# The bonus products of the chunked state stage write to bank XB0 in place of PB1

## The chip, the cores and the metric

The kernel runs on one core of a Trainium2 chip. The metric is the device time of one execution in microseconds; the number quoted is the median of several runs. The core's engines are named as the profile names them: PE is TensorE's matmul row and PEld its weight loads, DVE is VectorE, ACT is ScalarE, POOL is GpSimd, and SP is the queue that issues most of the transfers. Each engine works through its own list of instructions in order. They meet only at semaphores, counters on which one engine waits until another has raised them. Matmul results go to PSUM, which the kernel uses as banks of 128 partitions by 512 f32 values.

## The reference

One layer of a diffusion backbone over 2048 latent tokens and 256 context tokens of width 1024: a token mixer with two branches (retention and RWKV-7 time mixing, both in both directions), then a mixture of 16 experts. The change sits in the RWKV-7 branch. For every token `t` and each of 8 heads of width 64 the state is updated and read, and a per-head bonus is formed beside it:

```python
def step(s, xt):
    wt, kt, vt, kkt, at = xt[:5]
    sa = jnp.einsum('bhvk,bhk->bhv', s, -kkt)
    s = (s * wt[:, :, None, :] + sa[..., None] * (kkt * at)[:, :, None, :]
         + vt[..., None] * kt[:, :, None, :])
    ...
    return s, jnp.einsum('bhvk,bhk->bhv', s, xt[5])
...
u = lp['rwkv_w0'][:, None, None, :] + jnp.einsum('btr,drc->dbtc', jnp.tanh(wd), lp['rwkv_w2'])
a = jax.nn.sigmoid(lp['rwkv_a0'][:, None, None, :] + jnp.einsum('btr,drc->dbtc', ad, lp['rwkv_a2']))
...
bonus = jnp.sum(qu['r'][None] * st['k'] * r_k, axis=-1, keepdims=True).sum(0) * st['v']
```

The bonus is, for each token and head, a sum over the head's 64 channels of a product of three vectors. The kernel forms the product on POOL (`bon`) and takes the sum on PE, by a matmul against `ones2`, a matrix of two columns that mark the two heads of a block of 128 channels.

## The kernel before, in words

The function `rwkv_chunks` replaces the scan over tokens by work on chunks of 128 tokens. There are 18 chunks and two directions, so 36 halves. The prologue prepares the first chunk; then a loop of 18 passes runs two halves each (`d` = 0 and 1), and an epilogue finishes the last one. A half does two things at once. It inverts a triangular matrix for the chunk that was prepared, in six levels (`couple` and `double` on PE, `copies` on ACT, `levels` on DVE), and it prepares the next chunk of the other direction. The order on each engine is the order of the calls in its `body`, written out by hand. There is no planner; what an engine waits for is in its `wait_ge` calls.

All eight banks are in use: `XB[0]`, `XB[1]`, `TP[0]`, `TP[1]`, `TTP[0]`, `TTP[1]`, `PB[0]` and `PB[1]`. The end of a half and the start of the next one, which is what the change touches, go like this:

- On PE, `pairs` (L900) makes the products of the next chunk, two banks for each of four `q`: `XB`, then `PB`, then `XB` again, then `TTP`. DVE's `masked` (L778) empties each of the eight banks with one operation and raises `m1d` by one for it, so `m1d` 5 and 6 stand for the second use of `XB[0]` and `XB[1]`, and `m1d` 8 for all.
- PE's `turn` (L911) then transposes `beta` into `PB[0]`, `kappa` into `PB[1]` and `vS` into `PB[0]`. ACT's `turned` copies them out (`trc` 1, 2, 3).
- At the end of `turn`, PE sums the bonus (L916, eight small matmuls in the profile, since an f32 product takes two): it writes 8 columns of `PB[1]`, after waiting for `trc` 2 (the copy of `kappa_t` out of that bank) and for POOL's `bon`.
- PE's `low_rank` computes `u` into `PB[0]` (L874) and `a` into `PB[1]` (L879) for the chunk after the next. Before L879 it waits for `bonc`, which ACT raises when it has copied the 8 columns into `bo`.
- PE's `inverse_seed` starts the next half: for each group of four heads it adds `TTb` into `TP[g]` (L932) and `TTP[g]` (L934). DVE makes `TTb` in `seeds` (L782, L784) from ACT's copy `ATb`.
- PE's `couple` (L941) multiplies into `XB[0]` and `XB[1]`, each after ACT's copy `Tb` of that group.

On ACT the same stretch reads: `ATb` of group 0, `beta_t`, `kappa_t`, `v_t`, `ATb` of group 1, `bo`, then `rates` (a table load and the sigmoid `sg` out of `PB[0]`, and the sigmoid `av` out of `PB[1]`, L609 and L612), then `copies(0)`, the two copies `Tb`. All ACT copies have one line, L599. SP stores `bo` after `bonc` (L529).

Of the kernel before, what the change touches and what calls it, by code (L numbers as in the profile page):

```python
# [46 lines left out]
START = 1  # L47


class Room:  # L50
# [17 lines left out]
    def sb(self, name, shape, dt=F32):  # L68
        return self.stack.enter_context(self.nc.sbuf_tensor(f"{self.tag}__{name}", list(shape), dt))
# [4 lines left out]
    def sem(self, name, start=None):  # L74

        self.sems.append((self.nc.alloc_semaphore(f"{self.tag}__{name}"), self.start if start is None else start))
        return self.sems[-1][0]
# [334 lines left out]
def rwkv_chunks(nc, T):  # L412
# [11 lines left out]
    with Room(nc, "rwc") as room:  # L424
# [3 lines left out]
        ones2 = sb("ones2", [P, 2])  # L428
# [13 lines left out]
        sg, L, D, D2, e_bk, e_rho, e_al, av, kd, bb, bon = [sb(n, [P, 4, C]) for n in (  # L442
            "sg", "L", "D", "D2", "e_bk", "e_rho", "e_al", "av", "kd", "bb", "bon")]
# [13 lines left out]
        bo = sb("bo", [P, 8])  # L457
        XB, TP, TTP = [[room.ps(f"{n}{g}", [P, 512]) for g in range(NG)] for n in ("XB", "TP", "TTP")]
        PB = [room.ps(f"PB{u}", [P, 512]) for u in range(2)]
# [7 lines left out]
                 m1d=8, xb0=2, tt0=2, xd=12, ed=2, gd=6, hadd=1, hup=2,  # L467
# [3 lines left out]
        S = {n: sem(n) for n in N}  # L471
# [126 lines left out]
        def _(act):  # L598
            cp = lambda out, in_, n: act.activation(out, in_, ACT.Copy).then_inc(S[n], 1)  # L599
# [39 lines left out]
            def starts(d, at, ahead):  # L639
                def half(g):  # L640
                    act.wait_ge(S["m1d"], at("m1d", GH * g + GH, ahead) + START)
                    cp(ATb[:, g, :, :], BK[d][:, GH * g:GH * g + GH, 0, :], "atb")

                def turned(j):
                    act.wait_ge(S["trm"], at("trm", j + 1, ahead) + START)
                    cp((beta_t, kappa_t, v_t)[j][d][:, :], PB[j % 2][:, :], "trc")
                half(0)
                turned(0)
                turned(1)
                turned(2)  # L650
                half(1)
                act.wait_ge(S["bonm"], at("bonm", 1, ahead) + START)
                act.wait_ge(b_out, at("bonc", 0, ahead) * 16 + START)
                cp(bo[:, :], PB[1][:, 0:8], "bonc")

            def prologue(at):
                rates(0, at, 0)
                scale_bk(0, at, 0)
                scale_al(0, at, 0)
                scale_rho(0, at, 0)  # L660
                carry(0, at, 0)
                starts(0, at, 0)
                rates(1, at, 1)
# [29 lines left out]
            def body(i, d, at):  # L693
                e = 1 - d
                copies(0, at)
                copies(1, at)
                right_side(at)
                copies(2, at)
                copies(3, at)
                scale_bk(e, at, 1)  # L700
                copies(4, at)
                scale_al(e, at, 1)
                scale_rho(e, at, 1)
                carry(e, at, 1)
                copies(5, at)
                solved(at)
                act.wait_ge(S["gd"], at("gd", 6) + START)
                act.wait_ge(S["imt"], at("imt") + START)
                for g in range(NG):
                    act.wait_ge(S["tm"], at("tm", 11 + g) + START)  # L710
                    cp(T32[:, g, :, :], f4(TP[g]), "t32")
                outputs(at)
                for g in range(NG):
                    act.wait_ge(S["ttm"], at("ttm", 11 + g) + START)
                    cp(TT32[:, g, :, :], f4(TTP[g]), "tt32")
                act.wait_ge(S["sm"], at("sm", 1) + START)
                starts(e, at, 1)
                rates(d, at, 2)
# [145 lines left out]
        def _(pe):  # L864
            mm = pe.matmul
# [3 lines left out]
            def low_rank(d, at, ahead, i):  # L869
                pe.wait_ge(lds[d], i * (16 * NLD) + 16 * NLD + START)  # L870
                if ahead:
                    pe.wait_ge(S["trc"], at("trc", 0, ahead) + START)
                for q in range(4):
                    m = mm(f4(PB[0])[:, q, :], w2[:, d, q * P:q * P + P], wS[d][:, :], start=True, stop=True)  # L874
                m.then_inc(S["um"], 1)
                if ahead:
                    pe.wait_ge(S["bonc"], at("bonc", 0, ahead) + START)
                for q in range(4):
                    m = mm(f4(PB[1])[:, q, :], a2[:, d, q * P:q * P + P], aS[d][:, :], start=True, stop=True)  # L879
                m.then_inc(S["am"], 1)  # L880
# [23 lines left out]
            def turn(d, at, ahead):  # L904
                for j, src in enumerate((beta, kappa, ld[d]["vS"])):
                    if j < 2:
                        pe.wait_ge(S["m1d"], at("m1d", 3 + j, ahead) + START)
                    else:
                        pe.wait_ge(S["trc"], at("trc", 1, ahead) + START)
                    for q in range(4):  # L910
                        m = pe.transpose(f4(PB[j % 2])[:, q, :], src[:, q, :], ident[:, :])  # L911
                    m.then_inc(S["trm"], 1)
                pe.wait_ge(S["trc"], at("trc", 2, ahead) + START)
                pe.wait_ge(S["bonp"], at("bonp", 1, ahead) + START)
                for q in range(4):
                    m = mm(PB[1][:, 2 * q:2 * q + 2], bon[:, q, :], ones2[:, :], start=True, stop=True)  # L916
                m.then_inc(S["bonm"], 1)

            def prologue(at):
                low_rank(0, at, 0, 0)  # L920
                for q in range(4):
                    pairs(q, 0, at, 0)
                turn(0, at, 0)
                low_rank(1, at, 1, 0)
# [11 lines left out]

            def couple(l, at):
                for g in range(NG):
                    pe.wait_ge(S["tbc"], at("tbc", 2 * l + g + 1) + START)
                    for h in range(GH):  # L940
                        m = mm(f4(XB[g])[:, h, :], ATb[:, g, h, :], Tb[:, g, h, :], start=True, stop=True)  # L941
                    m.then_inc(S["xm"], 1)
# [80 lines left out]
            def body(i, d, at):  # L1023
                e = 1 - d
                inverse_seed(at)
                couple(0, at)
                right_side(e, at)
                double(0, at)
                errors(0, e, at)
                couple(1, at)  # L1030
                errors(1, e, at)
                double(1, at)
                outputs1(e, at)
                for l in (2, 3, 4):
                    couple(l, at)
                    refine(l - 2, 0, at)
                    double(l, at)
                    refine(l - 2, 1, at)
                couple(5, at)
                solve(at)  # L1040
                double(5, at)
                outputs2(e, at)
                pairs(0, e, at, 1)
                state(e, at)
                for q in range(1, 4):
                    pairs(q, e, at, 1)
                turn(e, at, 1)
                low_rank(d, at, 2, i + 1)
# [1821 lines left out]
```

## Time and profile before

| what | value |
|---|---|
| median of 3 runs | 5187.11 us (5186.87 to 5187.73) |
| profiled execution | 5195.17 us, of which the span is 5193.4 us |
| granted clock of PE, mean | 0.913 |
| instructions | 77499 |
| DVE busy | 2354.2 us (45%) |
| ACT busy | 1894.9 us (36%) |
| POOL busy | 513.3 us (10%) |

The profile records one execution. Its own time is 5195.17 us, 0.16% over the median of the runs. The changed stage takes the stretch from about 1440 to 2900 us of the span. Engines run side by side, so the busy shares don't add up to the span; what sets the time of a stage is the chain in which each piece starts when the one before it ends. In a timeline row the bracket at the end is the time the engine sat idle before the piece and the instruction that released it; a row without one started right behind the engine's previous work.

### The profile page before, as it was taken

The numbers are of one execution on the slowest core, as the hardware profiler recorded it, in microseconds if no ns is written. First come the engines' busy times: TensorE is split into PE (matmuls) and PEld (weight loads), VectorE is DVE, ScalarE is ACT, GpSimd is POOL, SyncE is SP. The second block draws the span as 40 slices with busy tenths as digits, with TensorE's granted clock in tenths as the row PEclk, the third lists the DMA queues.
The fourth block names the chain that finished last, engine by engine and source line by source line (L and its number), as shares of the span: only waits on it lengthen the run. The fifth ranks groups of instructions, "written<-read, shape, count | busy, mean of one in ns | idle before, by whom it ended". The sixth has DMA issues, their size and how long they took to land. (4 is left out here: it accounts for less than half of the span.)

```text
span 5193.4 us, 77499 instructions
## 1 busy us (share of the span) xinstructions
PE 4249.9 (82%) x28976; PEld 3593.1 (69%) x28976; DVE 2354.2 (45%) x3436; ACT 1894.9 (36%) x2727; POOL 513.3 (10%) x477
## 2 busy tenths in 40 slices
PE   7999999993169999999999356459883999999993
PEld 5788888882058888888888246347662888888882
DVE  4000000004756666666666535543445454454454
ACT  5111111113345665655655110110331444444443
POOL 0000000000121111111111002322000000000000
PEclk9999999997589999999999677569895999999996
DMA  7112122225621111111121454555633665666666
GB/s 268 65 66 79 64 73 73 73 73 181 224 78 53 44 52 51 44 56 47 44 58 44 167 177 133 153 172 183 207 129 149 217 209 210 219 210 214 216 208 267
DMA packets 397448, 681.54 MB, mean 131 GB/s; under 512 B 43436, under 2 KB 311316, under 8 KB 364984
## 3 DMA queue, kind: packets, MB, share of 16 engines
q1 hardware_dynamic: 376600, 577.60, 32.9%
q0 software_dynamic: 19488, 93.46, 5.6%
q10 hardware_dynamic: 1280, 9.44, 0.6%
q8 instruction: 47, 0.77, 0.1%
q14 instruction: 33, 0.27, 0.0%
HBM read 504.84 MB, written 175.58 MB: 131 GB/s over the span
## 5 line engine op out<-in xcount | busy, mean ns | idle before, releaser
L106 PE MATMUL zp__acc<-prh__hT_hi,zp__wh 128*128 128x512 f32 (+1 forms) x1616 | 615.0, 381 | 9.7 <-DVE zp__wl L2747 9.7
L107 PE MATMUL zp__acc<-prh__hT_hi,zp__wl 128*128 128x512 f32 (+1 forms) x1616 | 614.7, 380 | 0.0
L108 PE MATMUL zp__acc<-prh__hT_lo,zp__wh 128*128 128x512 f32 (+1 forms) x1616 | 614.4, 380 | 0.0
L2406 DVE TENSOR_TENSOR exp__wl<-exp__raw,exp__wh 128x4096 fp32r<-128x4096 f32 x97 | 429.1, 4424 | 332.1 <-ACT exp__wh L2358 332.1
L2747 DVE TENSOR_TENSOR zp__wl<-zp__w,zp__wh 128x1024 fp32r<-128x1024 f32 x48 | 58.8, 1226 | 1010.1 <-ACT zp__wh L2726 1010.1
L2358 ACT ACTIVATE exp__wh<-exp__raw 128x4096 fp32r<-128x4096 f32 x97 | 352.1, 3630 | 289.0 <-PE exp__acc L108 192.1
L2735 ACT ACTIVATE zp__zo<-zp__acc 128x512 f32<-128x512 f32 (+1 forms) x202 | 116.9, 579 | 884.1 <-PE zp__acc L108 884.1
L106 PE MATMUL exp__acc<-exp__wh,exp__xh 128*128 128x512 f32 x1024 | 402.3, 393 | 2.6 <-DVE exp__xl L2411 2.6
L108 PE MATMUL exp__acc<-exp__wl,exp__xh 128*128 128x512 f32 x1024 | 399.8, 390 | 0.0
L107 PE MATMUL exp__acc<-exp__wh,exp__xl 128*128 128x512 f32 x1024 | 399.6, 390 | 0.0
L106 PEld LDWEIGHTS zp__acc<-prh__hT_hi,zp__wh 128*128 128x128 f32 x1616 | 305.1, 189 | 67.7 <-DVE zp__wl L2747 10.0
L107 PEld LDWEIGHTS zp__acc<-prh__hT_hi,zp__wl 128*128 128x128 f32 x1616 | 305.2, 189 | 57.3
L108 PEld LDWEIGHTS zp__acc<-prh__hT_lo,zp__wh 128*128 128x128 f32 x1616 | 305.0, 189 | 57.6
L599 ACT ACTIVATE rwc__Tb<-rwc__TP 128x512 bf16<-128x512 f32 x432 | 234.7, 597 | 279.9 <-PE rwc__TP L950 279.9
L799 DVE TENSOR_TENSOR rwc__Xb<-rwc__XB,rwc__level 128x512 bf16<-128x512 f32 x432 | 277.0, 683 | 110.5 <-PE rwc__XB L941 110.5
L106 PEld LDWEIGHTS exp__acc<-exp__wh,exp__xh 128*128 128x128 f32 x1024 | 192.9, 188 | 44.6 <-issue 2.9
L108 PEld LDWEIGHTS exp__acc<-exp__wl,exp__xh 128*128 128x128 f32 x1024 | 192.9, 188 | 40.7
L107 PEld LDWEIGHTS exp__acc<-exp__wh,exp__xl 128*128 128x128 f32 x1024 | 193.0, 188 | 39.5
L106 PE MATMUL exp__acc<-exp__wh,exp__hh 128*128 128x512 f32 x512 | 203.7, 398 | 0.0
L108 PE MATMUL exp__acc<-exp__wl,exp__hh 128*128 128x512 f32 x512 | 200.0, 391 | 0.0
L107 PE MATMUL exp__acc<-exp__wh,exp__hl 128*128 128x512 f32 x512 | 199.5, 390 | 0.0
L808 DVE TENSOR_TENSOR rwc__Gr<-rwc__PB,rwc__TT 128x512 f32<-128x512 f32 x222 | 153.1, 690 | 97.1 <-PE rwc__PB L985 91.3
(420 smaller groups left out, 8326.7 us busy)
## 6 DMA issues: line engine op xcount, KB each, us to landing
exp__raw<-in_w_x SPq DMA_DIRECT2D x98, 2048.0 KB, 7.4
s_zT<-zp__zo SPq DMA_DIRECT2D x28, 1024.0 KB, 4.5
zp__w<-in_w_z SPq DMA_DIRECT2D x48, 512.0 KB, 5.3
s_zT<-zp__zo SPq DMA_DIRECT2D x18, 1152.0 KB, 5.0
brp__gate<-s_zT SPq DMA_DIRECT2D x20, 1024.0 KB, 8.7
nrm__w<-in_w_mod POOLq DMA_DIRECT2D x16, 1024.0 KB, 7.4
rch__X<-s_zT SPq DMA_DIRECT2D x14, 1024.0 KB, 6.8
rwc__kS<-s_kS SPq DMA_DIRECT2D x39, 256.0 KB, 3.0
```

Source lines behind the costliest of these rows:

```text
L106: pe.matmul(out, sh, mh, start=first, stop=False)
L107: pe.matmul(out, sl, mh, start=False, stop=False)
L108: return pe.matmul(out, sh, ml, start=False, stop=last)
L599: cp = lambda out, in_, n: act.activation(out, in_, ACT.Copy).then_inc(S[n], 1)
L799: tt(Xb[:, g, :, :], f4(XB[g]), level[:, d, l, None, :].to_broadcast([P, GH, C]), ALU.mult).then_inc(S["xd"], 1)
L808: tt(Gr[:, g, :, :], f4(PB[1]), TT32[:, g, :, :], ALU.add).then_inc(S["gd"], 1)
L2358: act.activation(wh[s][:, :, :], raw[s][:, :, :], ACT.Copy).then_inc(w_hi, 1)
L2406: ve.tensor_tensor(wl[s][:, :, :], raw[s][:, :, :], wh[s][:, :, :], ALU.subtract).then_inc(w_lo, 1)
L2735: act.activation(zo[u][:, lo:lo + n], acc[b][:, 0:n], fn).then_inc(kept, 1)
L2747: ve.tensor_tensor(wl[u][:, :, :], w[u][:, :, :], wh[u][:, :, :], ALU.subtract).then_inc(split_lo, 1)
```

## The change

The sum of the bonus goes to the first 8 columns of `XB[0]` in place of `PB[1]`. Four edits follow from it: PE's wait ahead of the sum is for `m1d` 6 in place of `trc` 2; ACT copies `bo` from `XB[0]`; PE's wait for `bonc` ahead of L879 is gone; and `couple`, which writes `XB[0]` next, waits for `bonc` before its first group at level 0. Below L875 the lines of PE's part move up by two, until the two lines added in `couple`.

```diff
@@ scalar: starts
                 act.wait_ge(S["bonm"], at("bonm", 1, ahead) + START)
                 act.wait_ge(b_out, at("bonc", 0, ahead) * 16 + START)
-                cp(bo[:, :], PB[1][:, 0:8], "bonc")
+                cp(bo[:, :], XB[0][:, 0:8], "bonc")
@@ tensor: low_rank
                 m.then_inc(S["um"], 1)
-                if ahead:
-                    pe.wait_ge(S["bonc"], at("bonc", 0, ahead) + START)
                 for q in range(4):
                     m = mm(f4(PB[1])[:, q, :], a2[:, d, q * P:q * P + P], aS[d][:, :], start=True, stop=True)
@@ tensor: turn
-                pe.wait_ge(S["trc"], at("trc", 2, ahead) + START)
+                pe.wait_ge(S["m1d"], at("m1d", 6, ahead) + START)
                 pe.wait_ge(S["bonp"], at("bonp", 1, ahead) + START)
                 for q in range(4):
-                    m = mm(PB[1][:, 2 * q:2 * q + 2], bon[:, q, :], ones2[:, :], start=True, stop=True)
+                    m = mm(XB[0][:, 2 * q:2 * q + 2], bon[:, q, :], ones2[:, :], start=True, stop=True)
@@ tensor: couple
                 for g in range(NG):
+                    if l == 0 and g == 0:
+                        pe.wait_ge(S["bonc"], at("bonc", 1) + START)
                     pe.wait_ge(S["tbc"], at("tbc", 2 * l + g + 1) + START)
```

The order of instructions on PE at the end of the first half of a pass, before. A row has the line, the operation, out<-in and, in brackets, the semaphores waited for; a semaphore may carry the name of an earlier stage that used the same one (`nrm__out` is `m1d` here, `rch__kkn_out` is `tt0`, the count of `TTb`, and `mod__silu_ok` the loads):

```order
L913 REGISTER_ALU
L916 MATMUL rwc__PB1<-rwc__ones2,rwc__bon 128x2 [waits rwc__bonp,rwc__trc]
L916 MATMUL rwc__PB1<-rwc__ones2,rwc__bon 128x2 x3
L870 ISA
L872 REGISTER_ALU [waits mod__silu_ok]
L874 MATMUL rwc__PB0<-rwc__wS0,rwc__w2 128x128 [waits rwc__trc]
L874 MATMUL rwc__PB0<-rwc__wS0,rwc__w2 128x128 x3
L879 MATMUL rwc__PB1<-rwc__aS0,rwc__a2 128x128 [waits rwc__bonc]
L879 MATMUL rwc__PB1<-rwc__aS0,rwc__a2 128x128 x3
```

The same place on PE in the changed kernel:

```order
L911 REGISTER_ALU
L914 MATMUL rwc__XB0<-rwc__ones2,rwc__bon 128x2 [waits rwc__bonp,nrm__out]
L914 MATMUL rwc__XB0<-rwc__ones2,rwc__bon 128x2 x3
L870 ISA
L872 REGISTER_ALU [waits mod__silu_ok]
L874 MATMUL rwc__PB0<-rwc__wS0,rwc__w2 128x128 [waits rwc__trc]
L874 MATMUL rwc__PB0<-rwc__wS0,rwc__w2 128x128 x3
L877 MATMUL rwc__PB1<-rwc__aS0,rwc__a2 128x128 x4
```

The sequence of matmuls is the same; the last group stands there without a wait of its own. Further on in the same list, past the seeds of group 0, PE comes to the seeds of group 1 and the first product of the next half. Before:

```order
L932 MATMUL rwc__TP1<-rwc__identb,rwc__TTb 128x128 [waits rch__kkn_out]
L932 MATMUL rwc__TP1<-rwc__identb,rwc__TTb 128x128 x3
L934 MATMUL rwc__TTP1<-rwc__TTb,rwc__identb 128x512 [waits nrm__out]
L939 REGISTER_ALU
L941 MATMUL rwc__XB0<-rwc__Tb,rwc__ATb 128x128 [waits rwc__tbc]
```

And in the changed kernel:

```order
L930 MATMUL rwc__TP1<-rwc__identb,rwc__TTb 128x128 [waits rch__kkn_out]
L930 MATMUL rwc__TP1<-rwc__identb,rwc__TTb 128x128 x3
L932 MATMUL rwc__TTP1<-rwc__TTb,rwc__identb 128x512 [waits nrm__out]
L939 REGISTER_ALU [waits rwc__bonc]
L941 MATMUL rwc__XB0<-rwc__Tb,rwc__ATb 128x128 [waits rwc__tbc]
```

The wait for `bonc` has moved here, onto a register instruction that stood here before.

On ACT, around the copy of the bonus in the same half (- before, + after):

```order
 L599 ACTIVATE rwc__ATb<-rwc__BK1 128x512 [waits nrm__out]
 L653 ISA [waits mod__w_in3]
-L599 ACTIVATE rwc__bo<-rwc__PB1 128x8 [waits rwc__b_out]
+L599 ACTIVATE rwc__bo<-rwc__XB0 128x8 [waits rwc__b_out]
 L607 REGISTER_ALU
 L609 ACT_TABLE_LOAD [waits rwc__dd2]
```

Only the bank that the copy reads is another (`mod__w_in3` is `bonm`); nothing on ACT changes place, and the other engines' lists are the same.

## Rows read from the trace of the kernel before

**Rows 1.** Busy time of the engines, from the page (share of the span, instructions)
```profile
PE 4249.9 (82%) x28976; PEld 3593.1 (69%) x28976; DVE 2354.2 (45%) x3436; ACT 1894.9 (36%) x2727; POOL 513.3 (10%) x477
```

**Rows 2.** Busy time by stretch (us), PEclk the granted clock as a share
```profile
1500.00:2000.00 500.00, 458.22 (x5133) 407.44 (x5132) 341.12 (x591) 298.05 (x553) 81.61 (x65) 1.00 0.18 50
...
2860.00:2900.00 40.00, 32.88 (x296) 28.56 (x294) 17.57 (x31) 11.19 (x20) 4.50 (x4) 0.90 0.17 48
```

**Rows 3.** Waits from 1440 to 2900 us: total us, times, longest
```profile
PE rwc__XB L941 <- ACT rwc__Tb L599: 30.3, 36, 0.9
...
PE rwc__PB L879 <- ACT rwc__bo L599: 23.5, 36, 0.7
```

**Rows 4.** ScalarE groups, same stretch: busy us, mean ns, idle before
```profile
L612 ACT ACTIVATE rwc__av<-rwc__PB 128x512 f32<-128x512 f32 x38 | 22.5, 592 | 0.0
...
L599 ACT ACTIVATE rwc__bo<-rwc__PB 128x8 f32<-128x8 f32 x37 | 5.9, 159 | 0.0
```

**Rows 5.** Timeline of one boundary between halves: start us, us, engine
```profile
2096.58 1.29 DVE L778 TENSOR_TENSOR rwc__BK<-rwc__XB,rwc__quad 128x512 f32<-128x512 f32 x2
...
2097.29 0.59 ACT L599 ACTIVATE rwc__kappa_t<-rwc__PB 128x512 f32<-128x512 f32 x1
...
2097.94 1.05 PE L916 MATMUL rwc__PB<-rwc__ones,rwc__bon 128*128 128x2 f32 x8
...
2098.14 0.60 ACT L599 ACTIVATE rwc__v_t<-rwc__PB 128x512 f32<-128x512 f32 x1 [0.26 <-PE rwc__PB L911]
...
2098.24 0.42 DVE L784 TENSOR_TENSOR rwc__TTb<-rwc__Xb,rwc__identb 128x512 bf16<-128x512 bf16 x1
...
2098.58 1.28 DVE L778 TENSOR_TENSOR rwc__BK<-rwc__TTP,rwc__quad 128x512 f32<-128x512 f32 x2
...
2098.85 1.14 PE L874 MATMUL rwc__PB<-rwc__wS,rwc__w 128*128 128x128 f32 x8
...
2099.90 0.63 ACT L599 ACTIVATE rwc__ATb<-rwc__BK 128x512 bf16<-128x512 f32 x1 [1.16 <-DVE rwc__BK L778]
...
2100.43 0.16 ACT L599 ACTIVATE rwc__bo<-rwc__PB 128x8 f32<-128x8 f32 x1
...
2100.61 1.28 ACT L609 ACT_TABLE_LOAD   x1
...
2100.64 0.97 PEld L879 LDWEIGHTS rwc__PB<-rwc__aS,rwc__a 128*128 128x128 f32 x8 [0.84 <-ACT rwc__bo L599]
...
2101.02 0.43 DVE L784 TENSOR_TENSOR rwc__TTb<-rwc__Xb,rwc__identb 128x512 bf16<-128x512 bf16 x1
...
2101.53 0.32 PEld L932 LDWEIGHTS rwc__TP<-rwc__identb,rwc__TTb 128*128 128x128 bf16 x4
...
2101.86 0.38 PE L934 MATMUL rwc__TTP<-rwc__TTb,rwc__identb 128*128 128x512 bf16 x1
...
2101.86 0.42 PEld L932 LDWEIGHTS rwc__TP<-rwc__identb,rwc__TTb 128*128 128x128 bf16 x4
...
2101.90 0.60 ACT L609 ACTIVATE rwc__sg<-rwc__PB 128x512 f32<-128x512 f32 x1
...
2102.30 0.38 PE L934 MATMUL rwc__TTP<-rwc__TTb,rwc__identb 128*128 128x512 bf16 x1
...
2102.40 0.59 ACT L612 ACTIVATE rwc__av<-rwc__PB 128x512 f32<-128x512 f32 x1
...
2102.87 1.09 ACT L599 ACTIVATE rwc__Tb<-rwc__TP 128x512 bf16<-128x512 f32 x2
...
2103.53 0.89 PE L941 MATMUL rwc__XB<-rwc__Tb,rwc__ATb 128*128 128x128 bf16 x8 [0.85 <-ACT rwc__Tb L599]
```

**Rows 6.** Timeline of the next boundary
```profile
2139.48 1.16 PE L879 MATMUL rwc__PB<-rwc__aS,rwc__a 128*128 128x128 f32 x8 [0.65 <-ACT rwc__bo L599]
...
2142.37 0.89 PE L941 MATMUL rwc__XB<-rwc__Tb,rwc__ATb 128*128 128x128 bf16 x8 [0.85 <-ACT rwc__Tb L599]
```

**Rows 7.** Timeline of the last boundary
```profile
2878.56 1.16 PE L961 MATMUL rwc__PB<-rwc__Hb,rwc__AR 128*128 128x128 f32 x8 [0.75 <-ACT rwc__sg L609]
```

## The prediction

> **What bounds the kernel now.** I read the page's busy times first. PE is the busiest engine, 82% of the span [rows 1]. That says nothing yet of this change, which sits in one stage and touches one spot of it, the boundary between two halves. So the next view was the windows by stretch: in the stage PE's row is busy 458.22 of 500 us, and the granted clock is 1.00, the 2.4 GHz level, until the last few microseconds [rows 2]. Then the waits: the one that the change removes, PE ahead of L879 for ACT's copy `bo`, is 23.5 us in total, 36 times, 0.65 us each. Right behind it in the table of waits stands another: PE ahead of L941 for ACT's copy `Tb`, 30.3 us, 36 times, 0.84 us each [rows 3]. Both belong to the same boundary, and the whole question is whether taking away the first makes the second shorter or longer.
>
> The timeline of one boundary answers it [rows 5]. Follow two engines.
>
> PE: the bonus sum starts at 2097.94, `u` (L874) at 2098.85, `a` (L879) at 2100.64 after a gap, the seeds of group 0 (loads at 2101.53, last product 2101.86 to 2102.24), the seeds of group 1 (loads at 2101.86, last product 2102.30 to 2102.68), and then PE is idle for 0.85 us until L941 starts at 2103.53.
>
> ACT: `ATb` of group 1 at 2099.90, released by DVE's last mask (2098.58 + 1.28 = 2099.86); `bo` at 2100.43; the table load at 2100.61; `sg` at 2101.90; `av` at 2102.40; the two `Tb` from 2102.87. Each of these starts where the one before it stops, or a tenth earlier since ACT overlaps neighbours. The pair of `Tb` takes 1.09 us with a step of about 0.5 us, so the first ends near 2103.46, and L941 starts 0.07 us after it.
>
> So the boundary's last chain is DVE's masks, then ACT from 2099.90 to 2103.46, then L941. PE is a side branch: it hands ACT its inputs and then waits. The ACT groups confirm that this is so in every half: idle time before `av` is 0.0 us in 38, before `bo` 0.0 in 37 [rows 4]. Neither ever waited for PE. The next boundary shows L879 at 2139.48 and L941 at 2142.37: 38.84 us later each, with the same 0.85 us ahead of L941 [rows 6]. The last boundary, in which the epilogue follows, has PE waiting 0.75 us ahead of L961, and again for ACT (`sg`) [rows 7].
>
> **The change part by part.**
>
> *The wait ahead of `a` goes.* PE comes to it when the weight loads of `u` are through: the loads of L879 started at 2100.64 after 0.84 us of idle, so that was at 2099.80 [rows 5]. (The 0.65 us of the waits is the same gap seen from the products, which end a little after their loads.) Nothing else holds `a`: `PB[1]` is free of `kappa_t` since 2097.29 + 0.59 = 2097.88 [rows 5]. So `a` moves 0.84 us forward. Its last product ended at 2101.80 or a little before, by the seeds that follow (loads at 2101.53); it will end at 2100.96. Who gains? `av` needs `a`, but `av` starts at 2102.40 behind `sg`, 0.60 us after `a` was done already. Gain on ACT: 0.
>
> *The seeds.* Group 0 moves 0.84 us forward with PE, its last product to 2101.02 to 2101.40; its inputs are there (`TTb` of group 0 done at 2098.24 + 0.42 = 2098.66, last mask 2099.86). Group 1 needs the second `TTb`, 2101.02 + 0.43 = 2101.45, so with the 0.05 us from an end to what it releases it can't load before 2101.50; it moves by 2101.86 - 2101.50 = 0.36 us, and ends at 2102.32 in place of 2102.68. `Tb` of group 0 reads `TP[0]`, complete at 2102.24 at the latest before, and starts at 2102.87: it had 0.63 us in hand, and now 1.48. Gain on ACT: 0 again.
>
> *What is late next.* L941 waits for `Tb`, still 2103.46, and starts at 2103.53 as before. Of PE's gaps, 0.65 us ahead of `a` becomes 0; PE then idles 0.3 to 0.5 us ahead of the seeds of group 1 (2101.50 against the end of the loads of group 0, 2101.53 + 0.33 - 0.84 = 2101.02 at the latest, so up to 0.5 us as its loads see it), and 0.85 + 0.36 = 1.21 us ahead of L941. The gap changes its place.
>
> *The new wait ahead of the sum.* It is for the sixth mask. The row that starts at 2096.58 holds masks five and six and ends at 2096.58 + 1.29 = 2097.87; the wait that it replaces was for `kappa_t`, 2097.88 [rows 5]. The difference is 0.01 us, and the sum stands behind the transposes of `vS` on PE either way. From below it is -0.01, from above 0.05 us (the step from an end to the start that it releases, `bo` 2100.59 to L879 2100.64). I take 0. And if it came late, there is cover: the sum is done at 2098.99, and `bo` reads it at 2100.43, 1.44 us later.
>
> *The copy `bo`.* The same shape (159 ns on the mean [rows 4]) out of another bank; nothing else touches `XB[0]` between the mask and L941. 0.
>
> *The new wait ahead of L941.* `bonc` is raised at 2100.59, 2.9 us before L941. It sits on a register instruction that PE ran there before, while PE idles; behind it in the queue stands only L941, which waits for `Tb` anyway. The cover is ACT's order itself, since `bo` is ahead of `Tb` on the same engine. 0; as an upper bound one release step more, 0.07 us, times 36 = 2.5 us.
>
> *Transfers.* SP's store of `bo` waits for the same copy, and its loads for `am` among others; `am` comes 0.85 us earlier but was raised a half ahead of SP's need. 0.
>
> *Sum.* 36 boundaries (35 and the last) times 0 = 0. The profiled execution's 5195.17 us stays 5195.17. It lies 8.06 us over the median of the runs, so the forecast is given against the median: 5187.1 us.
>
> **A rule against this.** PE is 82% busy, ACT and DVE well below [rows 1]. The Trainium skill, "Perfetto Trace Analysis", section "Optimization Strategy", says to take the engine that is most contended, find its gaps, and make what ends them come sooner; and that a gap which repeats can mean too little PSUM for the next tile. That fits the 36 gaps ahead of L879 to the letter, a bank held by eight columns. By that rule the sum would be 36 times 0.65 us off; by the rows on ACT it is nothing, because ahead of the next product PE waits for ACT a second time. The trace decides this case against it, as far as one profile can.
>
> **The rivals.**
>
> *1. PE's gap is paid out in full.* If PE bounded the boundary, 23.5 us would go [rows 3]: 5187.1 - 23.5 = 5163.6 us. For it: PE is the busiest engine, and the wait is a true wait. Against it: the 0.85 us that PE idles 1.7 us later, and ACT's 0.0 idle. A weaker form is that ACT's first `Tb` follows the seeds after all, by the 0.36 us that group 1 moves: 36 x 0.36 = 13 us, 5174 us. The same rows speak against it, since 0.63 us lay between.
>
> *2. Slower: the sum waits for the masks too long.* DVE has other work between the masks. If the sum were released not by the sixth but only by the last one, at 2099.86, it would start at 2099.91 in place of 2097.94, 1.97 us late, and end at 2100.96. `bo`, which ACT reaches at 2100.43, would start at 2101.01, and all ACT work behind it 0.58 us later, L941 with it: 36 x 0.58 = 21 us, 5208 us. It decides from 1.44 us of lateness on. Against it: the count waited for is 6 of 8, and the sixth mask ends 2 us before the last.
>
> *3. Slower by the clock.* The gap ahead of L941 grows from 0.85 to 1.21 us. In the stage the clock stayed at 1.00 with gaps of 0.85; where PE's work gets thin, after 2860 us, the granted clock is 0.90 on the mean of 40 us [rows 2]. If it fell once in each half to the 1.2 GHz level, for the group L941 and one f32 group like L874 (0.89 + 1.14 us [rows 5]), these would take up to twice as long: 2.0 us more, 36 x 2.0 = 73 us, 5260 us. Against it: PE's idle time in a half doesn't grow, it moves by 2 us.
>
> *4. The wait isn't really gone.* Another one ahead of L877, for the loads or for a bank, could hold `a` at its old time. The time would be that of the forecast, and only the trace would tell.
>
> **How the numbers follow.** About 0.2%, 10 us, is what a measurement of this kernel can tell from no change. Forecast 0.84, rival 4 another 0.03, both within 0.2%: 0.88 with a share for small shifts. Rival 1 in its two forms 0.07, all of it faster. Rival 2 has 0.02, rival 3 has 0.01, and 0.02 more is for a slower time by a cause that I don't see: 0.05 slower. The likeliest case's own spread is 2.5 us upwards by the waits, and some 3 us both ways by where the clock's steps fall in the stages behind, as runs of the same kernel differ by 0.9 us: 5183 to 5191. It holds over 8 in 10 without the rivals' times, so these stay outside.
>
> **What would show it.** In the new profile the wait of PE ahead of L877 for ACT `bo` is gone; the wait ahead of L941 for `Tb` grows from 30.3 to about 43 us over 36; ACT's idle before `av` and `bo` stays 0.0; a half still takes 38.84 us. The forecast is wrong if the half gets shorter: then either `av` or `Tb` was held by PE in a way that the idle column doesn't show. It is wrong to the other side if ACT idles before `bo`, or if the granted clock in the stage is under 1.00.

## The result, and the profile after

The changed kernel takes 5224.88 us (median of 6 runs, 5212.94 to 5233.27) against 5186.99 us of the kernel before on the same chips. The ratio is 1.0074, 95% interval 1.0063 to 1.0085: slower by 38 us, where no change was forecast. The profiled execution took 5222.04 us, its span 5220.3 us.

First the place. The copy `av` on ACT (L612) comes once in each half, so its first and last start bracket the stage. The first row is of the kernel before, the second of the one after (times are the first and the last start, us):

```profile
L612 ACT ACTIVATE rwc__av<-rwc__PB x38: 592/592/593, 1460.8 to 2878.4; 128x512 f32<-128x512 f32 x38
```

```profile
L612 ACT ACTIVATE rwc__av<-rwc__PB x38: 592/592/592, 1454.0 to 2911.1; 128x512 f32<-128x512 f32 x38
```

From first to last it was 1417.6 us and is 1457.1 us, 39.5 us more. The other stages of this profiled execution took 12.6 us less than in the one before, with the same instructions; that is within what executions of one kernel differ by (the kernel before ranged from 5176.72 to 5197.14 us over 31 later runs).

Next the waits of the stage, from 1440 to 2920 us (total us, times, longest), the answer to [rows 3]:

```profile
PE rwc__XB L941 <- ACT rwc__Tb L599: 50.3, 36, 1.4
```

PE's wait ahead of the `a` products is gone, and the one ahead of L941 has grown from 30.3 to 50.3 us over the same 36 (the prediction had about 43). The ACT groups, the answer to [rows 4] (busy us, mean ns, idle before):

```profile
L612 ACT ACTIVATE rwc__av<-rwc__PB 128x512 f32<-128x512 f32 x38 | 22.5, 592 | 0.0
...
L599 ACT ACTIVATE rwc__bo<-rwc__XB 128x8 f32<-128x8 f32 x37 | 5.8, 158 | 0.0
```

Still 0.0 us idle ahead of `av` and `bo`: PE kept ACT waiting at neither. The timeline of one boundary, the answer to [rows 5]:

```profile
2032.42 1.06 PE L877 MATMUL rwc__PB<-rwc__aS,rwc__a 128*128 128x128 f32 x8
...
2033.04 0.16 ACT L599 ACTIVATE rwc__bo<-rwc__XB 128x8 f32<-128x8 f32 x1
...
2034.11 0.40 PE L930 MATMUL rwc__TP<-rwc__identb,rwc__TTb 128*128 128x128 bf16 x4 [0.19 <-DVE rwc__TTb L784]
...
2034.34 0.38 PE L932 MATMUL rwc__TTP<-rwc__TTb,rwc__identb 128*128 128x512 bf16 x1
...
2035.00 0.59 ACT L612 ACTIVATE rwc__av<-rwc__PB 128x512 f32<-128x512 f32 x1
2035.48 1.09 ACT L599 ACTIVATE rwc__Tb<-rwc__TP 128x512 bf16<-128x512 f32 x2
...
2036.14 0.89 PE L941 MATMUL rwc__XB<-rwc__Tb,rwc__ATb 128*128 128x128 bf16 x8 [1.42 <-ACT rwc__Tb L599]
...
2036.92 1.15 PE L961 MATMUL rwc__PB<-rwc__Hb,rwc__AR 128*128 128x128 f32 x8
...
2037.91 1.90 PE L964 MATMUL rwc__PB<-rwc__v_t,rwc__BK 128*128 128x64 f32 x16
```

This is what the steps of the prediction said, line by line. L877 starts without a gap; the seeds of group 1 (L930) wait 0.19 us for `TTb`; `av`, `Tb` and L941 follow ACT. From `bo` to L941 it takes 2036.14 - 2033.04 = 3.10 us, and before it took 2103.53 - 2100.43 = 3.10. Only the gap ahead of L941 is 1.42 us and not the 1.21 of the prediction.

So where are 39.5 us? In the windows of the stage, the answer to [rows 2] (the column before the last two is the granted clock):

```profile
1500.00:2000.00 500.00, 458.20 (x4943) 408.30 (x4943) 329.22 (x572) 289.04 (x533) 77.83 (x62) 0.96 0.18 50
...
2500.00:2860.00 360.00, 329.82 (x3654) 293.39 (x3652) 240.00 (x417) 212.59 (x393) 59.02 (x47) 0.98 0.17 48
```

The clock was 1.00 in this stage and is 0.96 to 0.98. Cut at the starts of `av`, three halves in a row read:

```profile
1552.12:1592.49 40.37, 36.97 (x398) 33.11 (x398) 26.60 (x46) 23.27 (x45) 6.27 (x5) 0.96 0.17 49
1592.49:1634.49 42.00, 38.70 (x398) 34.77 (x398) 26.53 (x46) 23.37 (x45) 6.27 (x5) 0.92 0.16 45
1634.49:1673.32 38.83, 35.44 (x398) 31.51 (x398) 26.52 (x46) 23.25 (x44) 6.27 (x5) 1.00 0.18 50
```

The third has a length of 38.83 us and a clock of 1.00, as every half of the kernel before. The first two are 1.5 and 3.2 us longer, at 0.96 and 0.92. Of the 36 such intervals, 22 take 38.74 to 38.89 us, like all 36 before, and 14 take 40.31 to 43.17 us. The excess of the 14 adds up to 39.5 us, which is the whole loss. Below these 14 are called slow halves.

What happens in a slow half is in PE's timeline and in windows of 1 and 2 us, both of the second one:

```profile
1591.82 0.38 PE L932 MATMUL rwc__TTP<-rwc__TTb,rwc__identb 128*128 128x512 bf16 x1
1593.62 0.89 PE L941 MATMUL rwc__XB<-rwc__Tb,rwc__ATb 128*128 128x128 bf16 x8 [1.42 <-ACT rwc__Tb L599]
1594.40 1.75 PE L961 MATMUL rwc__PB<-rwc__Hb,rwc__AR 128*128 128x128 f32 x8
1595.95 3.51 PE L964 MATMUL rwc__PB<-rwc__v_t,rwc__BK 128*128 128x64 f32 x16
1599.26 0.63 PE L950 MATMUL rwc__TP<-rwc__Xb,rwc__TTb 128*128 128x128 bf16 x4
```

```profile
1592.00:1594.00 2.00, 0.58 (x5) 0.23 (x4) 0.31 (x1) 2.00 (x4) 0.00 (x0) 1.00 1.04 288
1594.00:1595.00 1.00, 0.91 (x9) 0.83 (x9) 0.94 (x2) 0.06 (x1) 0.00 (x0) 0.89 1.18 310
1595.00:1596.00 1.00, 1.00 (x7) 1.00 (x7) 1.00 (x2) 0.00 (x0) 0.00 (x0) 0.50 0.54 115
...
1601.00:1602.00 1.00, 1.00 (x9) 1.00 (x7) 0.00 (x0) 1.00 (x3) 0.00 (x0) 0.69 0.00 0
1602.00:1603.00 1.00, 0.83 (x12) 0.64 (x10) 0.58 (x1) 0.84 (x2) 0.00 (x0) 1.00 0.00 0
```

The clock falls to 0.50, the 1.2 GHz level, between 1594 and 1595, about 1.2 us after the gap of 1.42 us has ended, and stays there until past 1601. L941 still takes 0.89 us; L961 takes 1.75 us where it took 1.15 in the undisturbed half above, and L964 takes 3.51 us where it took 1.90. After that the half goes on at 2.4 GHz, with its delay.

The same holds for all of them. Between the first and the last start of `av` the trace of the changed kernel has 14 falls of the clock, one in each of the 14 slow halves and none in the other 22, and each begins 0.6 to 1.3 us after the start of L941. The trace of the kernel before has none there.

### The profile page after: what moved, and what is told of

Same layout as the page of the kernel before. It is cut to its first block and busy times, and to the rows that moved or that the text cites. A ratio compares the mean times of both kernels' runs of the same rounds, so it can differ in the third digit from the quotient of the medians.

```text
span 5220.3 us, 77499 instructions
## 1 busy us (share of the span) xinstructions
PE 4269.6 (82%) x28976; PEld 3617.1 (69%) x28976; DVE 2354.1 (45%) x3436; ACT 1896.2 (36%) x2727; POOL 513.5 (10%) x477
## 5 line engine op out<-in xcount | busy, mean ns | idle before, releaser
L599 ACT ACTIVATE rwc__TTb<-rwc__TTP 128x512 bf16<-128x512 f32 x360 | 196.9, 611 | 0.0
```

## The experiments

All ratios are to the kernel before, run on the same chip, with the 95% interval. Slow halves are counted in the profiled execution of each, the only one that has a trace, as intervals between starts of `av` of over 39.2 us.

**The old wait put back.** Sum in `XB[0]` with both new waits, and the wait for `bonc` ahead of L879 again:

```diff
+                if ahead:
+                    pe.wait_ge(S["bonc"], at("bonc", 0, ahead) + START)
                 for q in range(4):
                     m = mm(f4(PB[1])[:, q, :], a2[:, d, q * P:q * P + P], aS[d][:, :], start=True, stop=True)
```

> The bonus sum stays in XB0 with both new waits, and only PE's old wait for bonc ahead of the a product (L877) is put back. Theory: the changed kernel loses its time to the granted clock, because PE's two gaps at a boundary (0.65 us ahead of a, 0.85 us ahead of L941) have merged into one of 1.42 us ahead of L941; with the wait back the gaps are 0.65 and 0.85 us again, the clock is 1.00 in the whole stage and the time is that of the kernel before, 5187 us within 8. Rival: the bank itself costs (products of the sum in XB0, or the wait ahead of L941): then it stays near 5225 us, with halves over 38.9 us.

5188.94 us, ratio 0.9999 (0.9989 to 1.0009), 0 slow halves. The waits from 1500 to 2850 us:

```profile
PE rwc__XB L943 <- ACT rwc__Tb L599: 29.9, 35, 0.9
...
PE rwc__PB L879 <- ACT rwc__bo L599: 23.3, 35, 0.7
```

With the two gaps as they were (0.67 and 0.85 us on the mean) the loss is gone. The bank, the wait for `m1d` and the wait ahead of L941 cost nothing beyond the 0.1% of the interval. The removal of the wait is what made the kernel slower.

**PE's gap filled.** The changed kernel with four products that nobody reads:

```diff
                     if l == 0 and g == 0:
+                        for _ in range(4):
+                            mm(XB[1][:, :], identb[:, :], TTb[:, 1, :, :].rearrange("p h c -> p (h c)"), start=True, stop=True)
                         pe.wait_ge(S["bonc"], at("bonc", 1) + START)
```

> The changed kernel, with four products of 128x512 bf16 into XB1 (free at that point) put into PE's idle time ahead of the first L941 of each half; their results are overwritten. Theory of the clock: the gap ahead of L941 shrinks from 1.42 us to about 0.4, the clock stays at 1.00, the time is 5187 us within 8 although PE does 36 x 4 products more. Rival that the bank or the new wait costs: 5225 us or more. Rival that code placement made the change slow by chance: anything.

5189.51 us, ratio 1.0006 (0.9996 to 1.0015), 0 slow halves. PE's timeline at one boundary:

```profile
2017.84 0.40 PE L930 MATMUL rwc__TP<-rwc__identb,rwc__TTb 128*128 128x128 bf16 x4 [0.41 <-DVE rwc__TTb L784]
...
2018.29 1.03 PE L939 MATMUL rwc__XB<-rwc__TTb,rwc__identb 128*128 128x512 bf16 x4
2019.87 0.89 PE L943 MATMUL rwc__XB<-rwc__Tb,rwc__ATb 128*128 128x128 bf16 x8 [0.56 <-ACT rwc__Tb L599]
```

The filler takes the gap from 1.42 to 0.56 us, and 144 useless products take the time from 5224.88 back to 5189.51 us. (The 0.41 us ahead of the second L930 is 0.19 in truth: the records of L932's products of group 0 are missing in this trace, while the gap of the weight loads is the same 0.52 us as in the changed kernel's. The same holds for the next one and for those with one product and with fewer `a` products.)

**The gap cut in two.** The changed kernel with one product of two columns that waits for `av`:

```diff
                     if l == 0 and g == 0:
+                        pe.wait_ge(S["asg"], at("asg", 1, 1) + START)
+                        mm(XB[1][:, 0:2], identb[:, :], TTb[:, 1, 0, 0:2], start=True, stop=True)
                         pe.wait_ge(S["bonc"], at("bonc", 1) + START)
```

> The changed kernel, with one product of 2 columns into XB1 ahead of the first L941 that waits for ACT's av (asg), so PE's gap of 1.42 us is cut in two of about 0.8 and 0.5 us while its idle time in a half stays the same to 0.1 us. If the length of a single gap decides: clock 1.00 and 5187 us within 8. If the idle time of PE around the boundary decides, whatever its pieces: the clock still falls, in about as many halves, and the time stays within 5212 to 5233 us.

5195.94 us, ratio 1.0014 (1.0005 to 1.0024), 4 slow halves.

```profile
2029.84 0.40 PE L930 MATMUL rwc__TP<-rwc__identb,rwc__TTb 128*128 128x128 bf16 x4 [0.41 <-DVE rwc__TTb L784]
...
2031.38 0.18 PE L939 MATMUL rwc__XB<-rwc__TTb,rwc__identb 128*128 128x2 bf16 x1 [0.93 <-ACT rwc__av L612]
2031.88 0.89 PE L943 MATMUL rwc__XB<-rwc__Tb,rwc__ATb 128*128 128x128 bf16 x8 [0.31 <-ACT rwc__Tb L599]
```

Between the two expectations. Neither of the two pieces is over 0.93 us, and the clock still fell in 4 halves; but in far fewer than 14. The length of the longest gap isn't all of it, then. And the cut took 0.18 us off PE's idle time (0.19 + 0.93 + 0.31 for 0.19 + 1.42 us), where 0.1 was expected, so the run doesn't say what the cut by itself is worth.

**One gap without the bank.** The kernel before, with `a` between the two groups of seeds:

```diff
+                    if g == 1:
+                        low_rank_a(e, at, 1)
                     pe.wait_ge(S["tt0"], at("tt0", g + 1) + START)
```

(`low_rank_a` is the part of `low_rank` from the wait for `bonc` on, no longer called at its old place.)

> The kernel before (sum in PB1, a waits for bonc), with the a product moved behind the seeds of group 0, between them and those of group 1. The old gap ahead of a is filled by the seeds, and PE is idle in one piece of 1.1 to 1.4 us ahead of L941, as in the changed kernel, with no change of bank. Theory of the clock: falls in some of the halves, time 5200 to 5235 us, and halves without a fall take 38.8 us. Rival that the bank costs: 5187 us within 8.

5186.63 us, ratio 0.9986 (0.9976 to 0.9995), 0 slow halves.

```profile
2022.73 1.16 PE L881 MATMUL rwc__PB<-rwc__aS,rwc__a 128*128 128x128 f32 x8 [0.43 <-ACT rwc__bo L599]
2023.72 0.39 PE L937 MATMUL rwc__TP<-rwc__identb,rwc__TTb 128*128 128x128 bf16 x4
...
2025.62 0.89 PE L946 MATMUL rwc__XB<-rwc__Tb,rwc__ATb 128*128 128x128 bf16 x8 [1.29 <-ACT rwc__Tb L599]
```

A miss: the time is the one that was written down for the rival, that the bank costs. (The 0.14% under the kernel before isn't in the halves, which take 38.74 to 38.87 us as there.) The gap ahead of the first product of the half is 1.29 us, well over the 0.85 of the kernel before, and with the 0.43 us ahead of `a` PE's idle time is 1.72 us, more than the 1.61 us of the changed kernel. The clock stayed at 1.00. So neither a gap of 1.29 us by itself nor the idle time of the whole boundary brings it down.

Three things differ from the changed kernel: PE's idle time close ahead of the half is 1.29 us in place of 0.19 + 1.42, a full f32 group stands between the two gaps, and the sum is in `PB[1]`. The bank by itself isn't the cause, since with the sum in `XB[0]` and the old wait no half fell. Whether it has a part beside the gaps is not shown: all kernels with a fall have the sum in `XB[0]`, and none with `PB[1]` had more than 1.29 us of idle time close together.

**The same move in the changed kernel.** The edit is the one above, without a wait for `bonc`.

> The changed kernel with the a product moved between the seeds of the two groups. PE then has no gap ahead of the seeds of group 1 and one single gap of about 1.4 us ahead of L941, as long as in the changed kernel, but its idle time in the 2.2 us before L941 falls from 1.61 us to about 1.4. If the length of that one gap is what makes the clock fall: about as many slow halves as in the changed kernel (14 of 36), 5212 to 5233 us. [...]

5220.99 us, ratio 1.0068 (1.0053 to 1.0084), 11 slow halves.

```profile
PE rwc__XB L946 <- ACT rwc__Tb L599: 48.3, 34, 1.4
...
PE rwc__TP L935 <- DVE rwc__TTb L784: 6.6, 34, 0.2
```

The estimate of the idle time, 1.4 us, was wrong: the seeds of group 1 wait for DVE's `TTb` whatever PE does ahead of them, so 0.19 us stay and the sum is 1.61 us as in the changed kernel. The run therefore doesn't separate two readings, that the length of the one gap decides or that the idle time close together does. It does show that the same 1.61 us in another order of PE's work costs the same.

**One product of filler.** As the filled one, with `range(1)`.

> The changed kernel with one product of 128x512 bf16 (about 0.22 us) into XB1 at the start of PE's gap ahead of L941, where the run with four had no slow half. Idle time in the 2.2 us before L941 then is about 1.4 us (0.2 and 1.2). If idle time close together counts: 0 to 6 slow halves, 5187 to 5203 us, well under the 14 of the changed kernel. If the bank or the moved wait had a part in it after all: no change against 5225 us.

5205.18 us, ratio 1.0032 (1.0020 to 1.0044), 8 slow halves.

```profile
PE rwc__XB L943 <- ACT rwc__Tb L599: 41.0, 34, 1.2
```

0.22 us of work halve the loss. The slow halves are two more than I expected at most, and the time is 2 us over the range. And the single gap is 1.20 us, shorter than the 1.29 at which none fell (there with the sum in `PB[1]`): a second sign that the longest gap alone doesn't decide.

**More idle time.** The changed kernel with one of the four `a` products (so `a` is not the reference's from the second chunk on):

```diff
-                for q in range(4):
+                for q in range(4 if not ahead else 1):
                     m = mm(f4(PB[1])[:, q, :], a2[:, d, q * P:q * P + P], aS[d][:, :], start=True, stop=True)
```

> The changed kernel with three of the four a products left out from the second chunk on, so the a part is not the reference's there. PE does some 0.75 us less work per half just ahead of the seeds, which becomes idle time ahead of the seeds of group 1 (0.19 to about 0.9 us), with 1.42 us ahead of L941 as before. ACT's chain has the same length. Theory of the clock: more halves fall than the 14 of the changed kernel, 20 to 36, and the kernel gets slower by doing less: 5235 to 5320 us. Rival (the clock has nothing to do with idle time at this place, or PE's work bounds the half): 5225 us or less.

5258.19 us, ratio 1.0135 (1.0120 to 1.0151), 30 slow halves. The waits from 1500 to 2850 us:

```profile
PE rwc__XB L941 <- ACT rwc__Tb L599: 46.9, 33, 1.4
...
PE rwc__TP L930 <- DVE rwc__TTb L784: 35.5, 33, 1.1
...
PEld rwc__TP L930 <- DVE rwc__TTb L784: 39.3, 33, 1.2
```

The 1.1 us ahead of the second L930 hold 0.22 us of products of L932 whose records are missing here. The gap of the weight loads has grown by 1.19 - 0.52 = 0.67 us over the changed kernel's, so PE's is 0.19 + 0.67 = 0.86 us. Two halves with a fall, and one without:

```profile
1598.42:1640.42 42.00, 37.81 (x391) 34.10 (x392) 26.52 (x46) 23.37 (x44) 6.29 (x5) 0.92 0.17 45
1640.42:1680.57 40.15, 35.96 (x391) 32.30 (x392) 26.52 (x46) 23.26 (x45) 6.26 (x5) 0.96 0.17 48
...
1720.94:1759.82 38.88, 34.60 (x391) 30.84 (x392) 26.53 (x46) 23.26 (x44) 6.29 (x5) 1.00 0.18 50
```

PE does less, ACT's chain is the same, and the kernel is 73 us slower than the one before on the same chip. The clock accounts for it: the half shown without a fall still takes 38.88 us, and the 30 slow ones together are 65 us over that length.

Put together, with PE's idle time ahead of the seeds of group 1 and ahead of the first product of the half, in the order of the sum. (A gap ahead of `a`, 0.65 us before, 0.67 us with the old wait put back and 0.43 us in the kernel before with `a` between, lies at least the group `a` further back and isn't counted.)

| kernel | ahead of seeds 1 + ahead of L941, us | sum | slow halves | ratio |
|---|---|---|---|---|
| changed, four products of filler | 0.19 + 0.56 | 0.75 | 0 | 1.0006 |
| before | 0 + 0.85 | 0.85 | 0 | 1 |
| changed, old wait put back | 0 + 0.85 | 0.85 | 0 | 0.9999 |
| before, `a` between | 0 + 1.29 | 1.29 | 0 | 0.9986 |
| changed, one product of filler | 0.19 + 1.20 | 1.39 | 8 | 1.0032 |
| changed, gap cut | 0.19 + 0.93 + 0.31 | 1.43 | 4 | 1.0014 |
| changed, `a` between | 0.19 + 1.42 | 1.61 | 11 | 1.0068 |
| changed | 0.19 + 1.42 | 1.61 | 14 | 1.0074 |
| changed, three `a` products less | 0.86 + 1.42 | 2.28 | 30 | 1.0135 |

The idle time of PE that lies close together orders all of them but one pair (8 and 4). Chance in the counts is hardly the reason, since the medians over all runs order the pair the same way (1.0032 and 1.0014, with intervals that only just overlap). It may be that work in the middle of a gap counts for more than its length; these runs don't settle it. The counts of these two come from executions at the slow end of their runs (5211.49 and 5202.44 us), so the usual numbers are probably lower.

**A faster order.** The chain that bounds the boundary is ACT's, so the gain must come from there. `a` can stand between the seeds; those of group 0 are done early, and ACT can copy both `Tb` before the sigmoids. A sigmoid of one column puts the table load between the two copies:

```diff
@@ scalar: copies, for l == 0
+                        if g:
+                            act.activation(spare[:, :], ones2[:, 0:1], ACT.Sigmoid)
                         act.wait_ge(S["t0m"], at("t0m", g + 1) + START)
@@ scalar: body
                 copies(0, at)
+                rates(e, at, 1)
                 copies(1, at)
                 ...
                 starts(e, at, 1)
-                rates(d, at, 2)
```

The prologue's and the epilogue's calls of `rates` are moved to fit.

> A version that uses the moved wait for the engine that bounds the boundary: on PE the a product stands between the seeds of group 0 and 1, so the seeds of group 0 are done 1.5 us earlier; on ACT the copy Tb of group 0 goes ahead of the table load (placed by a one-column sigmoid), then Tb of group 1, and only then sg and av. ACT's chain from ATb to the second Tb loses sg and av (1.0 us), and the first product L941 can start about 1 us earlier with no long gap on PE. Expected by the theory: clock 1.00, a half of 38.1 to 38.4 us instead of 38.8, 5160 to 5178 us. If DVE's scan or PE's L961, which wait for sg, come last instead: 5187 us or up to 10 us more.

5167.62 us, ratio 0.9960 (0.9946 to 0.9973), 0 slow halves. One boundary, and the half that follows it:

```profile
2012.06 0.63 ACT L600 ACTIVATE rwc__ATb<-rwc__BK 128x512 bf16<-128x512 f32 x1 [1.15 <-DVE rwc__BK L781]
...
2012.65 0.59 ACT L600 ACTIVATE rwc__Tb<-rwc__TP 128x512 bf16<-128x512 f32 x1
...
2013.26 1.28 ACT L672 ACT_TABLE_LOAD   x1
...
2014.11 0.39 PE L949 MATMUL rwc__XB<-rwc__Tb,rwc__ATb 128*128 128x128 bf16 x4
...
2014.66 0.58 ACT L600 ACTIVATE rwc__Tb<-rwc__TP 128x512 bf16<-128x512 f32 x1
2015.14 0.59 ACT L610 ACTIVATE rwc__sg<-rwc__PB 128x512 f32<-128x512 f32 x1
...
2015.30 0.40 PE L949 MATMUL rwc__XB<-rwc__Tb,rwc__ATb 128*128 128x128 bf16 x4 [0.80 <-ACT rwc__Tb L600]
...
2015.86 1.15 PE L969 MATMUL rwc__PB<-rwc__Hb,rwc__AR 128*128 128x128 f32 x8 [0.17 <-ACT rwc__sg L610]
```

```profile
2015.62:2053.83 38.21, 35.31 (x399) 31.68 (x398) 26.62 (x46) 23.35 (x45) 6.28 (x5) 1.00 0.18 49
```

ACT's work is in the new order and the first product L949 of the half starts at 2014.11, 2.05 us after `ATb` (2012.06); in the kernel before it was 2103.53 - 2099.90 = 3.63 us. But the half gets only 0.62 us shorter (38.13 and 38.21 against 38.74 and 38.83), since the products of group 1 wait for the table load and L969 for `sg`. 36 times 0.62 is 22 us; the medians are 18 us apart here and 26 us in the run below.

**The faster order with the sum in `PB[1]`.** The same edits on the kernel before, beside the version above once more:

> The order of the version with the early Tb (a between the seeds, Tb of both groups ahead of sg and av), but with the bonus sum back in PB1, so a waits for bonc again. It tells what the change of bank is worth once ACT's order is the faster one. With the sum in PB1 the a products start about 0.4 us later, the seeds of group 1 some 0.2 us later, but Tb of group 1 has to wait for the table load anyway: a half of 38.15 to 38.4 us, 5165 to 5178 us. If a's start counts in full, 36 x 0.43 = 15 us over the same order with XB0.

> The version with the early Tb and the sum in XB0 once more, beside the one with PB1 on the same chip: 5160 to 5175 us, a half of 38.17 us, clock 1.00 in the stage.

With `PB[1]` 5163.34 us, 2 us below the range expected, ratio 0.9956 (0.9942 to 0.9969); with `XB[0]` 5163.02 us, ratio 0.9955 (0.9941 to 0.9968). Both have 0 slow halves and halves of 38.12 and 38.21 us. The waits with `PB[1]`:

```profile
PE rwc__XB L949 <- ACT rwc__Tb L600: 23.4, 35, 0.7
...
PE rwc__PB L884 <- ACT rwc__bo L600: 7.5, 35, 0.2
```

The wait ahead of `a` is back, 0.21 us each, and costs nothing that can be measured. Even in the order that was to make use of it the change of bank is worth 0: the medians are 0.3 us apart, where each interval reaches some 0.13% (7 us) to either side.

## Why the prediction was wrong

- *The wait ahead of `a` goes; the seeds move; what is late next.* Right. `a` starts without a gap, the seeds of group 1 are held by DVE, ACT idles 0.0 us ahead of `bo` and `av`, and a half that keeps its clock takes 38.74 to 38.89 us, unchanged. The gap ahead of L941 was sized too small, 1.21 for 1.42 us, since I moved the last product of the seeds by as much as its first load; in the new timeline the last product follows the first by 0.23 us, where it came 0.44 us behind the first load before.
- *The new wait ahead of the sum, the copy `bo`, the new wait ahead of L941: 0.* Right, shown by the run with the old wait put back: 0.9999.
- *"The gap changes its place", priced at nothing.* This is the step that failed: the prediction put the larger gap ahead of L941 into its sum at 0. A chain of waits has no price for idle time off the chain, but here PE's clock has. The moved gap cost 14 falls of the clock in 36 halves, 39.5 / 14 = 2.8 us each. The prediction had this as its third rival, at 2.0 us for each half, 73 us in all, with a chance of 0.01. The mechanism was right, a fall of the clock behind L941's gap; it struck in 14 halves and not in 36, and in the half shown it slowed not L941 (0.89 us as ever) but L961 and L964 behind it.
- *The argument against that rival*, "PE's idle time in a half doesn't grow, it moves by 2 us". True to 0.1 us (0.65 + 0.85 = 1.50 us, now 0.19 + 1.42 = 1.61 us) and beside the point. The move is what matters: before, 2.9 us with an f32 group and both seeds lay between the starts behind the two gaps [rows 5]; after, one gap of 1.42 us follows 0.19 us of another with only the seeds of one group between. The same work with its wait put back doesn't fall once.
- *The rule on the most contended engine*, and with it rival 1, would have given a gain of 23.5 us. It named the busiest engine rightly but not the one that bounds the boundary: with PE's order alone changed (the kernel before, `a` between) the ratio was 0.9986, with ACT's order changed too it was 0.9956.
- *Rivals 2 and 4* didn't occur: ACT idles 0.0 us ahead of `bo`, and `a` starts without a gap.
- The range ended at 5191 us. A rival with a mechanism and a row for it, the 0.90 of [rows 2], should have had more than 0.01, and a range that held it would have reached to about 5260 us.

The Trainium skill, "TensorE: Matmul & The Clock Gate", section "A second HAM failure mode: psum-queue depth-cycling", tells of another kernel in which PE idles briefly and often between groups that cycle through banks of PSUM, each matmul at its usual duration when the clock is up, and throughput lost to repeated falls. The trace agrees on the brief gaps and the repeated falls (L961 at 1.15 us with the clock up, 1.75 us in a fall, 14 falls in the stage). That cycling through banks has a part in it no run here shows: with the same banks and the old wait put back there was no fall. The prediction doesn't draw on this section.

What stays open: what exactly the chip counts. The falls order with idle time close together on PE, but one pair of runs does not fit, no kernel with the sum in `PB[1]` was run with as much of it, and why one half falls and the next, with the same rows, does not, is not explained here. Other work than this stage's wasn't tried.

## What to carry to other kernels

A wait removed off the critical chain need not be free when the engine is TensorE: look where its idle time lands, and whether it joins another gap. Read the clock per repetition and not per stage, since a clock of 0.97 on the mean was 22 repetitions unchanged and 14 with a fall. If a gap can't be closed by shortening the chain, cheap products in it can hold the clock, as four per half did here, but the real gain was in the order of the engine that the gap waits for.

## What the runs showed of the hardware that was not expected

- TensorE's clock fell to 1.2 GHz behind gaps of 1.2 to 1.4 us (1.42 us in the changed kernel, 1.20 us with one product of filler) in a stage in which PE is busy 92% of the time (458.20 of 500 us), for some 7 us in the half shown (from 1594 to 1601). Even with the gap cut into 0.93 and 0.31 us it fell in 4 of 36 halves.
- Leaving out three f32 products per half made the changed kernel slower (5258.19 us against 5224.88 us, ratios 1.0135 and 1.0074), and adding four useless bf16 products per half made it faster (5189.51 us, 1.0006).
- Whether the clock falls differs from half to half with the same rows: 14 of 36 halves in the changed kernel. The scatter of the runs doesn't show it: 20 us over 6 runs of the changed kernel (5212.94 to 5233.27), and 20 us over 31 runs of the kernel before (5176.72 to 5197.14).
